# Where a decode step's sliding-window cache copies are issued: a latent attention's page loop and one projection instead of nine stages

## The reference, cut to what matters

```python
for g, (win, dil) in enumerate(SWA_GROUPS):          # (128,1) (512,4) (2048,16)
    kv_new = qkv[:, :, 1:, g]
    prefix = zeros((B, win) + ...) if swa_past is None else swa_past[g]
    kv_g = concatenate([prefix, kv_new], axis=1)
    new_bufs.append(kv_g[:, -win:])                  # returned
```

## Time and profile before

| what | value |
|---|---|
| median of 3 runs | 3567.35 us |
| the profiled execution's own time | 3532.78 us |
| its span, first to last instruction | 3531.0 us |
| mean granted TensorE clock | 0.902 |
| TensorE matmul busy | 2905.3 us (82%) |
| moved by the DMA queues | 867.69 MB, mean 246 GB/s |
| all 48 copies of the sample windows | issued from 62 to 2197 us |

### The profile page before, as it was taken

The page is one execution under the profiler, slowest core; times in us unless marked ns, Lnnn a source line. Parts: engine busy times, 40 slices in busy tenths (PEclk is TensorE's granted clock), DMA queues, the critical chain, the costliest instruction groups (busy, mean ns, idle before and its releaser), DMA issues. The chain is left out here.

```text
span 3531.0 us, 45261 instructions
## 1 busy us (share of the span) xinstructions
PE 2905.3 (82%) x17313; PEld 2365.2 (67%) x17313; DVE 1506.6 (43%) x3598; ACT 544.0 (15%) x1380; POOL 611.7 (17%) x642
## 2 busy tenths in 40 slices
PE   6867778757666568999999997958776999999997
PEld 3434434535443338999989996724436999989997
DVE  1211100212110225997975552021115997985553
ACT  1223300234211221112100000000122112110000
POOL 0000040000000000433443330000000333444330
PEclk8668889879888688999999998978798999999998
DMA  3523272599754943898989995424253798989995
GB/s 115 199 90 105 63 229 101 161 296 285 210 201 159 318 142 121 332 380 308 347 323 409 409 409 199 177 86 177 95 186 133 281 383 303 348 312 410 409 409 210
DMA packets 275160, 867.69 MB, mean 246 GB/s; under 512 B 30625, under 2 KB 54210, under 8 KB 272423
## 3 DMA queue, kind: packets, MB, share of 16 engines
q1 hardware_dynamic: 198932, 593.14, 48.0%
q0 software_dynamic: 76032, 271.88, 20.4%
HBM read 846.23 MB, written 109.08 MB: 271 GB/s over the span
## 5 line engine op out<-in xcount | busy, mean ns | idle before, releaser
L2065 PE MATMUL ps<-xT,p0e_uT 128*128 128x192 f32 x2048 | 346.2, 328 | 8.9 <-DMA p0e_uT<-in_peer_uT 8.2
L2065 PE MATMUL ps<-xT,p1e_uT 128*128 128x192 f32 x2048 | 346.0, 328 | 8.8 <-DMA p1e_uT<-in_peer_uT 8.1
L2091 PE MATMUL ps<-p1e_S,p_qT 128*128 128x192 f32 x2048 | 337.4, 327 | 5.6 <-DMA p_qT<-in_peer_v 5.6
L2065 PEld LDWEIGHTS ps<-xT,p0e_uT 128*128 128x128 f32 x2048 | 333.9, 191 | 12.0 <-DMA p0e_uT<-in_peer_uT 10.6
L2065 PEld LDWEIGHTS ps<-xT,p1e_uT 128*128 128x128 f32 x2048 | 333.9, 191 | 11.7 <-DMA p1e_uT<-in_peer_uT 10.3
L2091 PE MATMUL ps<-p0e_S,p_qT 128*128 128x192 f32 x2048 | 337.0, 327 | 5.4 <-DMA p_qT<-in_peer_v 5.4
L2091 PEld LDWEIGHTS ps<-p1e_S,p_qT 128*128 128x128 f32 x2048 | 332.9, 190 | 10.0 <-DMA p_qT<-in_peer_v 9.9
L2091 PEld LDWEIGHTS ps<-p0e_S,p_qT 128*128 128x128 f32 x2048 | 332.8, 190 | 9.5 <-DMA p_qT<-in_peer_v 9.5
L1869 DVE SCALAR_TENSOR_TENSOR h_tok<-p0e_rows,p0e_dots,h_tok 128x1024 f32<-128x1024 f32 x127 | 163.1, 1285 | 141.9 <-DMA p0e_rows<-in_peer_v,p0e_expert 140.6
L1869 DVE SCALAR_TENSOR_TENSOR h_tok<-p1e_rows,p1e_dots,h_tok 128x1024 f32<-128x1024 f32 x127 | 163.2, 1285 | 140.4 <-DMA p1e_rows<-in_peer_v,p1e_expert 139.4
L1759 POOL DMA_INDIRECT p0e_rows<-in_peer_u,p0e_expert x128 | 153.1, 1196 | 393.8 <-DVE p0e_dots L1858 205.7
(11 more groups left out here) (456 smaller groups left out, 3821.0 us busy)
## 6 DMA issues: line engine op xcount, KB each, us to landing
p_qT<-in_peer_v SPq DMA_DIRECT2D x256, 512.0 KB, 7.3
p0e_uT<-in_peer_uT SPq DMA_DIRECT2D x128, 512.0 KB, 6.7
p1e_uT<-in_peer_uT SPq DMA_DIRECT2D x128, 512.0 KB, 6.8
out_swa_sample<-in_cache_swa_w SPq DMA_DIRECT2D x32, 2040.0 KB, 31.5
m_cache<-in_cache_mem_kv SPq DMA_DIRECT2D x32, 1024.0 KB, 5.5
ms_pages<-in_cache_mla SPq DMA_DIRECT2D x128, 144.0 KB, 2.5
ss_kcache<-in_cache_swa_w SPq DMA_DIRECT2D x72, 256.0 KB, 12.3
ss_vcache<-in_cache_swa_w SPq DMA_DIRECT2D x72, 256.0 KB
```

The costliest lines, as they stand in the source:

```text
L2065: mm = pe.matmul(k.ps[:, SB[i % len(SB)], 0:TD], ur[:, i % NU, c, :], k.xT[:, c, D0:T], start=(c == 0), stop=(c == KC - 1))
L2091: mm = pe.matmul(k.ps[:, c // 2, c % 2 * TD:(c % 2 + 1) * TD], vr[:, i % NV, c * P:(c + 1) * P], S[:, i, :], start=False, stop=(i == STEPS ...
```

## The change

- The 24 transfers of group 2 that hold the first three pieces (510 rows each) of every sequence leave the list. `copy_of_sequence` issues them in `mls`, three behind the loads of each sequence.
- The list of the other 40 is reordered: group 0, the 16 writes of zeros, group 1, the last piece of group 2 of every sequence.
- `qs` issues 8 (group 0) as before, `mlp` 16 (zeros, instead of 8 of group 1), `win` 16: two behind each of its loads from the third to the tenth. No other stage issues any.
- `gemm_stage`'s loads are written out, without a loop on SP, in every projection.

```diff
+COPY_ROWS, COPIED_IN_LOOP = 510, 3
...
                 for r in range(0, rows, step):
+                    if w == SWA_GROUPS[2][0] and r < COPIED_IN_LOOP * step:
+                        continue
...
-        return pieces + zero_rows
+        return pieces[:DEC_B] + zero_rows + pieces[DEC_B:]
...
+    def copy_of_sequence(self, eng, u):
+
+        for r in range(0, COPIED_IN_LOOP * COPY_ROWS, COPY_ROWS):
+            dst = self.io["swa_sample2"][0, ds(u, 1), r:r + COPY_ROWS].rearrange("b w c h d -> (b w) (c h d)")
+            src = self.io["cache_swa_w2048"][0, ds(u, 1), r + DEC_S:r + DEC_S + COPY_ROWS]
+            eng.dma_start(dst, src.rearrange("b w c h d -> (b w) (c h d)")).then_inc(self.copied, 16)
...
                         sp.dma_start(slot_view(s, kc, chunk), src).then_inc(landed[s], 16)
-                load(0)
-                if base == 0:
-                    k.copy_some(sp, copies)
-                if pairs > 1:
-                    with sp.Fori(1, pairs) as i:
-                        load(i)
+                        if n < len(copies):
+                            k.copy_some(sp, copies[n])
+                for i in range(pairs):
+                    load(i)
...
                     a["load_values"](sp, u, slot, v_landed[slot])
+                    if a.get("copy"):
+                        a["copy"](sp, u)
...
-        k.copy_some(sp, 8)
+        k.copy_some(sp, 16)
         sp.wait_ge(self.taken, len(self.chunks))
...
-        self.k.copy_some(sp, self.copies)
         sp.wait_ge(self.sem, self.due)
...
-                ], tables, copies=4)
+                ], tables, copies=(0, 0) + 8 * (2,))
...
+            "copy": k.copy_of_sequence,
...
-            ], copies=8)
+            ])
```

More of the change, by code:

```diff
@@ L217, in _, with gemm_stage @@
                                ACT.Copy).then_inc(bank_free, 1)
-def gemm_stage(k, name, jobs, beside=None, copies=0):
+def gemm_stage(k, name, jobs, beside=None, copies=()):
     nc = k.nc
@@ L1122, with __init__ @@
 class Stores:
-    def __init__(self, k, begin, sem, due, copies):
-        self.k, self.begin, self.sem, self.due, self.copies = k, begin, sem, due, copies
+    def __init__(self, begin, sem, due):
+        self.begin, self.sem, self.due = begin, sem, due
     def sync(self, sp):
         self.begin(sp)
-        self.k.copy_some(sp, self.copies)
         sp.wait_ge(self.sem, self.due)
@@ L1226, in even_mixer @@
                 attend_prompt(k, "swp", units, 3 * SEQ, 1.0, SWA_SCALE, Stores(
-                    k, lambda sp: store_windows(k, kv, sp), k.window_stored, 16 * N_WINDOW_STORES, 9))
+                    lambda sp: store_windows(k, kv, sp), k.window_stored, 16 * N_WINDOW_STORES))
             swa_sample(k, e, swa_qT, kT)
@@ L1471, in memory_attention @@
             attend_prompt(k, n_ + "p", units, N_MEM, MEM_SCALE, 1.0, Stores(
-                k, lambda sp: sp.dma_start(io["mem_kv_prompt"][layer, 0].rearrange("(i p) c h d -> p i (c h d)", p=P),
+                lambda sp: sp.dma_start(io["mem_kv_prompt"][layer, 0].rearrange("(i p) c h d -> p i (c h d)", p=P),
                                         mkv[:, :, :]).then_inc(k.mem_kv_stored, 16),
-                k.mem_kv_stored, 16 * (layer + 1), 8))
+                k.mem_kv_stored, 16 * (layer + 1)))
         with ExitStack() as c1:
@@ L1528, in odd_mixer @@
         cT = k.sb(ctx, "c_convT", [P, 8, T])
-        gemm_stage(k, "cin", [("feat", k.xT, io["conv_w_in"][0], 512, prod[:, :, :].rearrange("p a t -> p (a t)"))],
-                   copies=8)
+        gemm_stage(k, "cin", [("feat", k.xT, io["conv_w_in"][0], 512, prod[:, :, :].rearrange("p a t -> p (a t)"))])
         with ExitStack() as c1:
@@ L1548, in _ @@
                 sp.dma_start(taps[:, :], io["conv_w"][0]).then_inc(landed, 16)
-                k.copy_some(sp, 3)
                 sp.wait_ge(tail_taken, 2)
@@ L2162, in _ @@
                 k.copy_some(act, len(k.copies))
-                act.wait_ge(k.copied, 16 * len(k.copies))
+                act.wait_ge(k.copied, 16 * (len(k.copies) + DEC_B * COPIED_IN_LOOP))
 def constants():
```

## The result

| | before | after |
|---|---|---|
| median of 4 runs each, in turn on one chip | 3566.70 us (3546.03 to 3568.51) | 3515.93 us (3504.03 to 3523.38) |
| ratio, with its 95% interval | | 0.9868 (0.9821 to 0.9914): faster by 1.3% |
| the profiled execution | 3532.78 us | 3504.03 us |
| its span, granted clock | 3531.0 us, 0.902 | 3502.2 us, 0.905 |

The account below looks back on a forecast made before the run. TensorE was taken to idle for needed loads queued behind copies on SP's in-order queue. Gains of 69.3 us less costs of 6, 7.8 and 15.2 gave 40.3 off 3567.35: 3527.0 us, range 3506 to 3549.

Parts of the forecast that it names:

- Steps 1 and 2: Idle before `sws` falls from 33.44 to 7.2 us, gaining 26.2; layer 0's memory attention gains 43.1 us.
- Steps 3 and 4: `cin`, convolution, `m1in` lose copies and zeros, gain 0; `mlp` issues 16 zero writes instead of 8 copies, cost 0.
- Step 5: Loop of `mls`: pages plus three copies need 27.0 us per 26.0 us period; six periods cost 6 us.
- Step 6: End of `mls`: last two sequences' six copies delay `mv`'s weights; TensorE waits 7.8 us more than its 4.36.
- Step 7: `win`: second pair gains 5.8 us; loads behind two copies cost 10 in pairs, 11 in last chunks; net cost 15.2 us.
- Cheap covers: Copies run at 350 GB/s: `mls` loop pays 0, its end 4, `win` 10; net 55, 3512 us; chance 0.18.
- Late pages: Page loads in `mls` land late, their idle doubles, 24 us instead of 6; net 22, 3545 us; chance 0.20.
- Slow mix: Copies between pages in `mls` run at 259 GB/s, period 32.1 us; slower than before, 3585 us; chance 0.04.
- Not the copies: Layers differ by something else (clock, cache loads); only `sws` gains: 3570 us, no change; chance 0.03.

Follow-up runs that it names:

- the repeat: The changed kernel once more, unaltered, for a second trace, compared with the kernel before: 3506.93 us, ratio 0.9874.

## Why the prediction was right, point by point

It was right in sign, mechanism and range: 3515.9 us against 3527.0 (3506 to 3549), 1.3% against 1.1%. Where it was off, two costs were mis-sized in opposite directions, `win` 9.5 us too dear and the loop 4 too cheap; that the sum came within 7 us owes something to that luck.

| step | forecast | measured |
|---|---|---|
| 1, hole before `sws` | -26.2 | -25.2 (stages), -27 (copies alone taken out) |
| 2, memory attention of layer 0 | -43.1 | -42.6, -43 by time when its copies alone were taken out |
| 3 and 4, `cin` to `m1in`, `mlp` | 0 | +1 and -3 (stages), within scatter |
| 5, loop of `mls` | +6 | +10 |
| 6, end of `mls` | +7.8 | +8 |
| 7, `win` | +15.2 | +5.7 |
| sum | -40.3 | -44 (stages), -47 by the ratio (-31 to -64) |

**Steps 1 and 2** held within 1 us in the mean. In the first trace the hole was 10.68 us and not 7.2; in the repeat it was 6.72, and in the nine experiments with at most four copies ahead of it 6.65 to 8.34, so 10.68 was the exception. The nearest row, layer 1's first load with nothing ahead of it, was the right measure. That layer 1 is what layer 0 becomes was an argument; taking the 16 copies out alone showed it.

**Steps 3 and 4** were costed at nothing. The traces bear out step 3: from the start of `cin` to the output projection of `m1out` the kernel before takes 414.1 and 410.7 us, the changed kernel 413.6 and 414.0. The 7 us by which the first pair differs in the expert layers are scatter, for the two traces of the kernel before differ there by 16. Step 4 is within 3 us: TensorE's first work in `mls` comes at 225.6 and 227.9 us before, 222.6 and 225.7 after.

**Step 5** had the right mechanism and a term mis-sized. "Together 27.0 us of DMA for a period of 26.0" rested on both rates at a full share. Measured is a period of 27.9 and 28.0 us, where it was 26.0 and 26.9: not 1.0 but 1.5 us longer in the mean, and 1.9 against the trace that the forecast started from. The loop moves at 304 GB/s, with a share of 0.94. The share is lost while TensorE waits for pages; windows of one period, the wait and the rest:

```profile
289.86:296.58 6.72, 0.00 (x0) 0.00 (x1) 1.51 (x6) 0.00 (x0) 0.00 (x0) 0.64 0.66 204
296.58:318.78 22.20, 20.58 (x162) 12.74 (x162) 3.73 (x10) 9.36 (x17) 0.73 (x4) 0.88 1.02 334
```

The run with two copies showed the other side of it: when they have landed before the next pages are asked for, the copies cost nothing.

**Step 6** was right to a few tenths in the first trace: 7.8 us more than 4.36 makes 12.2, and it is 12.11 (13.31 in the repeat); `mv`'s weights were asked for 40.1 us after the last pages, forecast 40.0. Some of that is luck. The last copy landed 50.2 us after the last pages were asked for, not 47.8. The weights then landed 1.2 us behind it, where the sum keeps the whole wait of the kernel before, in which they took 3.6 us from issue to landing.

**Step 7** is the one that failed. It put a wait of 3.2 us and 1.8 us of slower clock into each pair; the waits are 1.35 and 1.28 (0.32 and 1.19 in the repeat). The step took half of 29.57 us as the time of the pair's first half. But the slow part of a pair lies in that half: 15.76 and 16.63 us, and 14.00 for the second. TensorE wants the load 1 us and more later than I had it; and load, two copies and load took 7.99 + 17.11 = 25.1 us in the second pair and 25.8 in the third (24.7 and 24.9 in the repeat), not 26.0. Behind the short waits no clock was lost. Windows of the changed kernel, the first and second half of the second pair, then the chunks behind the waits of 1.25 and of 4.24 us:

```profile
516.80:532.50 15.70, 15.70 (x32) 6.65 (x32) 0.00 (x0) 0.00 (x0) 0.00 (x0) 0.89 0.93 327
533.91:547.80 13.89, 13.89 (x32) 5.99 (x32) 0.00 (x0) 0.00 (x0) 0.00 (x0) 1.00 0.62 224
...
624.85:638.00 13.15, 13.15 (x48) 9.04 (x48) 0.00 (x0) 0.00 (x0) 0.00 (x0) 1.00 0.91 307
642.28:657.10 14.82, 14.82 (x48) 9.98 (x48) 0.00 (x0) 0.00 (x0) 0.00 (x0) 0.88 0.95 344
```

The granted clock is 0.89 behind the pair's pause of 7.99 us, 1.00 behind 1.35 and 1.25, and 0.88 behind 4.24. In those four chunks the waits sum to 6.1 us and the slow stretches to 2, 8.2 together where the step had 11. The second pair gave back 5.8 us, as said.

**The rivals.** *Cheap covers* had `win` right (10 - 5.8 is 4, measured 5.7) and the loop wrong: it would pay nothing. *Late pages* had the loop's waits at 8 us; they are 6.0, nearer to the forecast's 5. Part of its mechanism, pages behind the remains of copies, is what the landings show. The other part, a loaded memory, no run isolates: with two copies a sequence the copies had landed when the pages were asked for. The Trainium skill's figure for device memory at high load ("DMA: Bandwidth & Descriptors", section "Latency and other measured facts"), by which I had put some 11 us on the six sequences, is therefore neither borne out nor refuted here. *Slow mix* did not come: its period was 32.1 us, measured 27.9. The kernel with ACT's copies has a period near it, 33.3 us, but its copies land as fast as on SP's queue, so that is no sign of the rival's mechanism. *Not the copies* is refuted by the run without `m0in`'s and `m0p`'s.

**What was not foreseen** is the scatter. I took the 34.6 us between the profiled execution and the median as a constant. The second profile of the kernel before is 44 us longer than the first, and 20.5 of them lie in the loop of `sws` alone. The forecast's bounds on the steps were sound; the spans of a single pair of traces (-28.8) would have made me doubt them for a wrong reason.

## What to carry to other kernels

A background transfer on an in-order queue costs what the next needed load behind it is late, so ask of every place how long until that load is wanted, and fill it to below that: two copies a sequence cost nothing, three cost 18 us (10 in the periods, 8 at the end), and four behind the second load of a pair cost less than two behind each. A queue of their own was no way out here: issued later and from ACT, the same copies lost the whole gain. Before one trace is set against another, take a second one of the same kernel and compare stage by stage: here one loop varied by 20 us between two traces of one kernel, nearly half of what the change was worth.

## What the runs showed of the hardware

- The same loads of the `sws` loop ran at 266 GB/s in one execution and at 242 in another, with the DMA engines busy to 0.96 and 0.94. Over 14 traces the loop took 209 to 242 us. The cause was not found.
- Page loads asked for while copies of another queue were under way were late in their data and in their issue: with ACT's copies landing 7.4 to 9.4 us after the asking, 16 page loads took 15.3 us to issue, not 8.8, and TensorE idled 11.2 us (mean of six) for them instead of 6.0.
- Copies on SP's queue delayed the pages behind them only while they had not landed: with the last copy landed 0.8 to 2.4 us before the asking (0.1 after it once in six), TensorE waited 4.3 us (mean of six), as with no copies (4.25); with it landing 1.8 to 5.6 us after, 6.0.
